# First attention's q and k produced with tokens on the partitions, head norms and rotation along the free axis, moving weights realigned

## The chip, the cores and the metric

The kernel runs on one core of a Trainium2 chip. The metric is the device time of one execution in microseconds. The kernel before took 2663.46 us (median of 3 runs, 2660.84 to 2664.37).

## The reference

Two transformer-like layers follow each other on one sequence of 256 tokens with 2048 features, in float32. What matters here is the first layer's attention. The hidden state is normalised and multiplied by `w_in`; the first 3072 output features are q, k and v, 16 heads of 64 features each. Every head of q and k is normalised and its first 16 features are rotated by an angle that depends on the token:

```
h = rms_norm(x, g_mix)
q, k, v, z, xbc, dt_raw = split(h @ w_in)
q = partial_rope(rms_norm(q, g_q), positions) * 64 ** -0.5      # norm over the 64 features of a head
k = partial_rope(rms_norm(k, g_k), positions)
partial_rope: x1, x2 = x[:8], x[8:16] of each head; [x1*cos - x2*sin, x2*cos + x1*sin, x[16:]]
```

The masked softmax of q k^T over three window patterns follows, then `w_out`. Beside the attention runs a state-space branch (SSD) made from z, xbc and dt. Cross attention, an MLP and the whole second layer come after it.

## The kernel before

**Weights.** All large matmuls go through one stream of 907 granules. A granule is a weight tile of 256 input features by 512 output features (128 partitions x 1024 floats, 512 KB). It is loaded into one of five `raw` buffers seven granules ahead; ScalarE copies it rounded into `WH` (`high`), VectorE writes the rest `raw - WH` into `WL` (`low`, line 1901); both are rings of four slots. The activations have the same two halves, `XH` and `XL`. Each product is three fp32r matmul passes: XH with WH, XL with WH, XH with WL.

**Two forms of a granule** (`gran`, line 933). In the narrow form the weights are stationary (128x128) and the 256 tokens are moving: 24 matmuls of 256 columns; the result has output features on the partitions. In the wide form, used for v, w_cv and v2, the tokens are stationary (two blocks of 128) and 512 weight columns are moving: 12 matmuls of 512 columns; the result has tokens on the partitions. A narrow slot of the ring spreads its 256-float blocks 288 floats apart; a wide one (`flat_slot`, line 702) is contiguous from the slot's start, and slots are 1120 floats apart, so wide weights start at 0, 96, 64 or 32 floats past a multiple of 128.

**Order of work.** `make_plan` (line 324) gives each granule a slot of time and each side step a due slot. `chain` (line 198) places a row of dependent steps in consecutive slots, later when PSUM banks (`B`, four of them) or scratch tiles (`T`, eight) are taken. Each engine's loop goes through the slots, and within a slot through the steps in a fixed written order. On TensorE the granule comes first and then the side steps; on VectorE `low` comes first, then among others softmax steps, `qk_rope`, `qk_gain`, `qk_rs`, `qk_scale`, then `ssm_gain`, `ssm_rs`, `ssd_out`, `ssd_mask`. So each engine waits in its own order, and a step that is late holds everything written behind it.

**q and k before.** Chunks q,0 k,0 v,0 q,1 k,1 v,1 take slots 49 to 96, eight granules each. Per chunk there are two units of 256 features by 256 tokens, eight units j = 0 to 7. A unit's steps: `qk_scale` (VectorE: PSUM times the norm row), `qk_sq` (ScalarE: squares), `qk_sum` (TensorE: four small fp32 matmuls that sum 64 partitions), `qk_rs` (VectorE: inverse root by 12 small operations), `qk_wide` (ScalarE) and `qk_spread` (TensorE: four transposes that spread the roots over the partitions), `qk_gain` (VectorE), `qk_rot` (TensorE: an fp32 matmul of 512 columns with a rotation matrix) and `qk_rope` (VectorE: three operations of 512 elements). The first units stand in slots 57 to 63. The SSD steps stand beside them: the mask of unit 6 (`ssd_mask`) and its two heads' matmuls (`ssd_y`, which wait for it) in slot 58, those of unit 7 in slot 62.

Of the kernel before, what the change touches and what calls it, by code (L numbers as in the profile page):

```python
# [15 lines left out]
RING = 4  # L16
# [3 lines left out]
SLOT = 4 * BLOCK + 3 * 32  # L20
EPS = 1e-6
# [9 lines left out]
def cst_layout():  # L31
    names = [("ident", 128), ("tri", 128), ("ones", 128), ("tri2", 128), ("blk", 2), ("rot64", 128),
             ("dup", 128), ("rotdup", 128),
             ("mult", 384), ("causal", 384), ("invf", 1), ("pad", 3)]
    out, at = {}, 0
    for n, w in names:
        out[n] = (at, w)
        at += w
    return out, at


def col_layout():
    names = [("conv_w", 64), ("conv_b", 16), ("lru_ba", 16), ("lru_bi", 16), ("ffn_wg", 132), ("ffn_bg", 44),
             ("g_mix", 16), ("g_q", 1), ("g_k", 1), ("g_attn_out", 8), ("d_skip", 8),
             ("g_ssm_out", 8), ("g_cross", 16), ("g_mem", 16), ("g_cq", 1), ("g_ck", 1), ("g_mlp", 16),
             ("dt_bias", 16), ("a_log", 16), ("rnn_w", 64), ("rnn_b", 16), ("lru_lam", 16), ("ln1_g", 16),
             ("ln1_b", 16), ("ffn_wu", 132), ("ffn_bu", 44), ("ln2_g", 16), ("ln2_b", 16)]
    out, at = {}, 0
    for n, w in names:
        out[n] = (at, w)  # L50
        at += w
    return out, at
# [6 lines left out]
    "hn_scale": "qk_scale", "hn_rs": "qk_rs", "hn_gain": "qk_gain", "lam_x": "dt_x", "lam_one": "dt_one",  # L59
    "lam_end": "dt_end", "xr_taps": "xbc_taps", "gr_poly": "xs_mul", "gr_gelu": "cb_mask", "gr_mul": "z_scale",  # L60
    "rn_mul": "z_silu", "at_mul": "ssd_mask", "mg_lo": "ms_lo", "up_sq": "ssd_out", "up_lo": "xbc_silu",
    "dn": "xbc_scale", "qi_rope": "qk_rope", "kw_ki": "dt_acs", "rq": "ssm_gain", "lru_la": "ssm_rs",
# [6 lines left out]
    "up_hi": "z_tanh", "gr_sq": "ssd_exp", "gr_tanh": "ssm_sq", "rn_tanh": "ms_hi", "at_tanh": "qk_wide",  # L69
    "gt_tap": "xr_tap", "ln_hi": "rn_tanh", "ix_relu": "rope_sin_act", "lru_sqrt": "rope_cos_act", "ln_meanrow": "mg_hi",  # L70

    "hn_sum": "qk_sum", "hn_spread": "qk_spread", "ln_meanrow_pe": "xs_pe", "qi_rot": "qk_rot", "kw_pe": "dt_rows", "ix_qk": "cb_pe",
# [4 lines left out]
def granules():  # L77
# [33 lines left out]
    for r, (c0, n) in enumerate(ROUNDS):  # L111
# [3 lines left out]
        for c in range(4):  # L115
# [10 lines left out]
         "ssm_spread", "qk_sum", "qk_spread", "qk_rot", "sm_qk", "sm_tr", "sm_av", "hn_sum", "hn_spread", "qi_rot",  # L126
# [197 lines left out]
def make_plan():  # L324
# [231 lines left out]
def program(nc, A):  # L556
# [4 lines left out]
    with ctx:  # L561
# [130 lines left out]
        def slot(x, g):  # L692

            a = (g % RING) * SLOT
            return x[:, a:a + SLOT]

# [5 lines left out]
        def flat_slot(g):  # L702

            return width(g) < GRAN or P.grans[g][0] in ("v", "w_cv", "v2")
# [26 lines left out]
        def width(g):  # L731
            return weights(g)[1]
# [4 lines left out]
        def qk_of(j):  # L737

            return (qT, kT)[j // 2 % 2], 2 * (j // 4) + j % 2
# [30 lines left out]
        def sync(e):  # L770
# [21 lines left out]
            for t in range(P.slots):  # L792
# [32 lines left out]
        def tensor(e):  # L825
# [19 lines left out]
            def pair_over(job, c):  # L845
# [7 lines left out]
                elif job in ("q", "k"):  # L853
                    on.wait_ge(*s("qk_scale", 4 * c + (2 if job == "q" else 4)))
# [78 lines left out]
            def gran(g):  # L933
# [26 lines left out]
                elif job in ("v", "w_cv", "v2"):  # L960
# [120 lines left out]
            def qk_sum(j):  # L1081
                out, sq = S("qk", j), T("qk", j)
                on.wait_ge(*s("qk_sq", j + 1))
                free_S(on, "qk", j)
                for i in range(2):
                    for k in range(2):
                        a = k * 4 + i * 2
                        m = mm(out[:, a:a + 2], sq[:, i * 256 + k * 128:i * 256 + k * 128 + 128], C("blk"))
                m.then_inc(s["qk_sum"], 1)

            def qk_spread(j):
                out, wide = S("qk", j), T("qk", j)
                on.wait_ge(*s("qk_wide", j + 1))
                for i in range(2):
                    for k in range(2):
                        a = k * 4 + i * 2
                        m = tr(out[:, i * 256 + k * 128:i * 256 + k * 128 + 128], wide[:, a * 64:a * 64 + 128])
                m.then_inc(s["qk_spread"], 1)

            def qk_rot(j):  # L1100
                on.wait_ge(*s("qk_gain", j + 1))
                mm(S("qk", j)[:, :], C("rot64"), pair(*qk_of(j))).then_inc(s["qk_rot"], 1)


            def sm_qk(u):
                if u < 8:
                    on.wait_ge(*s("qk_rope", 3 + u // 2 % 2 + 4 * (u // 4)))
# [150 lines left out]
            for t in range(P.slots):  # L1258
# [36 lines left out]
                for u in P("qk_rot", t):  # L1295
                    qk_rot(u)
                for u in P("qk_spread", t):
                    qk_spread(u)
                for u in P("qk_sum", t):
                    qk_sum(u)  # L1300
# [19 lines left out]
        def scalar(e):  # L1320
# [118 lines left out]
            def qk_sq(j):  # L1439
                free_T(on, "qk", j)  # L1440
                on.wait_ge(*s("qk_scale", j + 1))
                fn(T("qk", j)[:, :], pair(*qk_of(j)), ACT.Square).then_inc(s["qk_sq"], 1)

            def qk_wide(j):
                on.wait_ge(*s("qk_rs", j + 1))
                fn(T("qk", j)[:, :].rearrange("p (c d) -> p c d", d=64),
                   root(5 + j % 4)[:, 0:8].unsqueeze(2).to_broadcast([128, 8, 64]), ACT.Copy).then_inc(s["qk_wide"], 1)
# [278 lines left out]
            for t in range(P.slots):  # L1726
# [82 lines left out]
                for u in P("qk_wide", t):  # L1809
                    qk_wide(u)  # L1810
# [75 lines left out]
        def vector(e):  # L1886
# [218 lines left out]
            def rope_angle(_):  # L2105
                a = T("rope")[:, 0:256]
                free_T(on, "rope")
                on.wait_ge(s["pos"], 16)
                e.tensor_copy(a, cosA[:, :].bitcast(I32)).then_inc(*own.up())
                on.wait_ge(*own.now)  # L2110
                ts(a, a, C("invf"), None, ALU.mult).then_inc(s["rope_angle"], 1)

            def reduced(out, turn):

                a, k = T("rope")[:, 0:256], T("rope")[:, 256:512]
# [27 lines left out]
            def qk_scale(j):  # L2143
                x, p = qk_of(j)
                on.wait_ge(s["gemm"], P.count("qk"[j // 2 % 2], j // 4))
                tt(x[:, 2 * p:2 * p + 2, :], two(bank("qk"[j // 2 % 2], j // 4, j % 2)), twice(rb[:, 0, :]),
                   ALU.mult).then_inc(s["qk_scale"], 1)

            def qk_rs(j):
                on.wait_ge(*s("qk_sum", j + 1))  # L2150
                rsqrt(root(5 + j % 4)[:, 0:8], S("qk", j)[:, 0:8], 8, 1.0 / 64, EPS).then_inc(s["qk_rs"], 1)

            def qk_gain(j):
                x = pair(*qk_of(j))
                on.wait_ge(*s("qk_spread", j + 1))
                stt(x, x, V(("g_q", "g_k")[j // 2 % 2]), S("qk", j)[:, :], ALU.mult, ALU.mult).then_inc(s["qk_gain"], 1)
# [410 lines left out]
            for t in range(P.slots):  # L2567
# [108 lines left out]
                for u in P("qk_rope", t):  # L2676
                    qk_rope(u)
# [4 lines left out]
                for u in P("qk_scale", t):  # L2682
                    qk_scale(u)
# [52 lines left out]
def constants():  # L2736
# [14 lines left out]
    put("blk", (i[:, None] // 64 == np.arange(2)[None, :]).astype(np.float32))  # L2751
# [45 lines left out]
    put("invf", table(64, 8)[:, None])  # L2797
# [67 lines left out]
```

## Time and profile before

| | |
|---|---|
| median of 3 runs | 2663.46 us |
| the profiled execution's own time | 2664.01 us |
| its span | 2662.2 us |
| TensorE busy | 2640.7 us |
| VectorE busy | 1775.5 us |
| ScalarE busy | 1337.8 us |
| GpSimd busy | 112.5 us |
| q and k stretch, 158 to 333 us: TensorE, VectorE busy | 174.53, 138.77 us |

Busy time of matmuls is not their rate: they are pipelined, so a matmul that is shown as 0.28 us can start every 0.11 us. The distance from start to start is what counts. A row of the list in order of time has the start, the time covered, engine, line, operation, output <- inputs and, in brackets, idle time ahead of it.

### The profile page before, as it was taken

The page shows a single profiled execution, that of the slowest core. Times are in us where ns is not written, and L with a number is a line of the kernel's source. Part 1 is how long each engine was busy: PE and PEld are TensorE (multiplying, and loading weights), DVE is VectorE, ACT ScalarE, POOL GpSimd, SP SyncE. Part 2 cuts the span into 40 slices and gives each one's busy share as a digit, 9 for nine tenths or more (in the row PEclk, how much of TensorE's full clock was granted, in tenths as well). Part 3 has the DMA queues.
Part 4 walks back from the last instruction along what each step waited for, and adds up shares of the span by engine and source line. Part 5 has one row for each costly group of instructions (what it writes and reads, how often), then busy time and mean ns, then how long its engine had stood idle before and what let it go on. Part 6 is the DMA issues. An engine that isn't in the chain of part 4 may idle for free.

```text
span 2662.2 us, 52796 instructions
## 1 busy us (share of the span) xinstructions
PE 2640.7 (99%) x22474; PEld 2591.6 (97%) x22474; DVE 1775.5 (67%) x2594; ACT 1337.8 (50%) x1817; POOL 112.5 (4%) x76
## 2 busy tenths in 40 slices
PE   9999999999999999999999999999999999999998
PEld 9998899899999999999899999999999999999997
DVE  7787779675555555565787786556676656665666
ACT  6474575554344443444445774444455435543553
POOL 2000021010000000000000000000300000000003
PEclk9999999999999999999999999999999999999999
DMA  7544546466666566665554556665566666666663
GB/s 254 181 143 151 177 157 189 150 207 192 196 192 197 191 195 193 196 192 178 166 167 153 178 180 194 194 195 183 150 199 192 196 193 196 192 196 192 197 191 103
DMA packets 137179, 488.45 MB, mean 183 GB/s; under 512 B 15344, under 2 KB 18288, under 8 KB 136944
## 3 DMA queue, kind: packets, MB, share of 16 engines
q1 hardware_dynamic: 136656, 484.82, 57.8%
q8 instruction: 176, 2.88, 0.5%
q14 instruction: 59, 0.48, 0.1%
q10 hardware_dynamic: 288, 0.26, 0.0%
HBM read 482.93 MB, written 2.10 MB: 182 GB/s over the span
## 4 chain that ended last, share of the span: by engine, by line
PE 94%; DVE 4%; ACT 1%; issue 0%; DMA 0%; SPq 0%; POOL 0%; ACTq 0%; DVEq 0%
PE ps L830 93%; DVE WL L1891 1%; PE ps L833 1%; DVE XL L1899 1%; DVE xT L1891 1%; DMA raw<-in_w_in 0%; ACT WH L1325 0%; DVE T L1891 0%; DVE XL L1891 0%; ACT xT L1325 0%; DVE T L1899 0%; DVE small L1899 0%; SPq L783 0%; DVE AL L1899 0%; ACT XH L1325 0%
## 5 line engine op out<-in xcount | busy, mean ns | idle before, releaser
L1891 DVE TENSOR_TENSOR WL<-raw,WH 128x1024 fp32r<-128x1024 f32 (+1 forms) x910 | 1123.6, 1238 | 755.2 <-ACT WH L1325 754.7
L1325 ACT ACTIVATE WH<-raw 128x1024 fp32r<-128x1024 f32 (+1 forms) x910 | 961.7, 1058 | 1265.0 <-PE ps L830 1261.9
L830 PE MATMUL ps<-XH,WH 128*128 128x256 f32 x5024 | 1401.2, 279 | 5.7 <-DVE WL L1891 3.6
L830 PE MATMUL ps<-XL,WH 128*128 128x256 f32 x5024 | 1389.5, 277 | 0.0
L830 PE MATMUL ps<-XH,WL 128*128 128x256 f32 x5024 | 1389.5, 277 | 0.0
L830 PEld LDWEIGHTS ps<-XH,WH 128*128 128x128 f32 x5024 | 943.1, 188 | 13.0 <-issue 11.6
L830 PEld LDWEIGHTS ps<-XL,WH 128*128 128x128 f32 x5024 | 943.3, 188 | 2.0 <-issue 1.2
L830 PEld LDWEIGHTS ps<-XH,WL 128*128 128x128 f32 x5024 | 942.9, 188 | 0.3
L830 PE MATMUL ps<-AH,WH 128*128 128x256 f32 x1856 | 513.0, 276 | 0.6 <-DVE AL L1891 0.4
L830 PE MATMUL ps<-AL,WH 128*128 128x256 f32 x1856 | 512.3, 276 | 0.0
L830 PE MATMUL ps<-AH,WL 128*128 128x256 f32 x1856 | 512.3, 276 | 0.0
L830 PEld LDWEIGHTS ps<-AH,WH 128*128 128x128 f32 x1856 | 348.4, 188 | 1.0 <-DVE AL L1891 0.6
L830 PEld LDWEIGHTS ps<-AL,WH 128*128 128x128 f32 x1856 | 348.4, 188 | 0.0
L830 PEld LDWEIGHTS ps<-AH,WL 128*128 128x128 f32 x1856 | 348.4, 188 | 0.0
L1842 POOL TENSOR_TENSOR T<-T 128x512 f32<-128x512 f32 (+1 forms) x50 | 77.6, 1555 | 490.6 <-ACT T L1325 489.3
L1842 POOL TENSOR_TENSOR T<-xT 128x512 f32<-128x512 f32 x2 | 2.6, 1308 | 1986.2 <-ACT T L1325 1986.2
L1899 DVE SCALAR_TENSOR_TENSOR T<-ps,cols,T 128x254 f32<-128x254 f32 (+2 forms) x186 | 76.8, 474 | 0.0
L1325 ACT ACTIVATE T<-ps,cols 128x256 f32<-128x256 f32 x120 | 56.5, 529 | 0.0
L1325 ACT ACTIVATE T<-ps 128x512 f32<-128x512 f32 (+2 forms) x110 | 55.7, 536 | 0.1
L830 PE MATMUL ps<-WH,XH 128*128 128x512 f32 x96 | 39.7, 414 | 0.0
L1325 ACT ACTIVATE T<-T 128x256 f32<-128x256 f32 (+1 forms) x94 | 39.7, 470 | 0.1
L830 PE MATMUL ps<-WL,XH 128*128 128x512 f32 x96 | 37.8, 394 | 0.0
(235 smaller groups left out, 1587.0 us busy)
## 6 DMA issues: line engine op xcount, KB each, us to landing
raw<-in_w_up SPq DMA_DIRECT2D x304, 512.0 KB, 4.3
raw<-in_w_in SPq DMA_DIRECT2D x223, 512.0 KB, 3.5
raw<-in_w_down SPq DMA_DIRECT2D x216, 512.0 KB, 4.3
raw<-in_w_out SPq DMA_DIRECT2D x64, 512.0 KB, 3.5
raw<-in_w_gates SPq DMA_DIRECT2D x64, 512.0 KB, 3.5
raw<-in_w_ckv SPq DMA_DIRECT2D x16, 512.0 KB, 3.6
raw<-in_w_cq SPq DMA_DIRECT2D x8, 512.0 KB, 4.4
raw<-in_w_co SPq DMA_DIRECT2D x8, 512.0 KB, 3.3
```

What stands on the lines that cost most here:

```text
L830: return e.matmul(out, l, r, start=start, stop=True, skip_group_check=True)
L833: return e.transpose(out, x, C("ident")[0:n, 0:n])
L1325: return e.activation(out, x, func, **kw)
L1842: return e.tensor_tensor(out, a, b, ALU.add)
L1891: return e.tensor_tensor(out, a, b, op)
L1899: return e.scalar_tensor_tensor(out=out, in0=a, scalar=x, in1=b, op0=op0, op1=op1)
```

## The change

q and k join v in the wide form, so they come out with tokens on the partitions, and a unit becomes 128 tokens by 512 features (8 heads). The sum over a head's 64 features is then a reduction along the free axis, on VectorE; the root is a value per partition and head; the rotation works on the first 16 features of each head, with tables of 32 values instead of 256 per partition. Four transposes bring the unit back to features on the partitions. The step list of a unit shrinks from nine to five. `qk_scale`, `qk_sum`, `qk_wide`, `qk_spread`, `qk_rot` and `qk_rope` are gone, `qk_tr` and `qk_copy` are new. The start of a wide slot of full size moves by `FLAT_AT`, so that it is 96 floats past a multiple of 128 in all four ring slots, for v, w_cv and v2 as well. The constants and columns tables change size (1670 to 1680 and 748 to 874 floats per partition), which shifts every tile placed behind them.

```
+FLAT_AT = (96, 0, 32, 64)
...
-        rope.append(P.chain(t, j, ("qk_scale", "qk_sq", "qk_sum", "qk_rs", "qk_wide", "qk_spread", "qk_gain", "qk_rot",
-                                   "qk_rope"),
-                            (T, ("qk", j), "qk_sq", "qk_rope"), (B, ("qk", j), "qk_sum", "qk_rope")))
+        rope.append(P.chain(t, j, ("qk_sq", "qk_rs", "qk_gain", "qk_tr", "qk_copy"),
+                            (T, ("qk", j), "qk_sq", "qk_tr"), (B, ("qk", j), "qk_tr", "qk_copy"), apart=("qk_tr",)))
...
+            if flat_slot(g) and width(g) == GRAN:
+                a += FLAT_AT[g % RING]
+                return x[:, a:a + GRAN]
...
-            return width(g) < GRAN or P.grans[g][0] in ("v", "w_cv", "v2")
+            return width(g) < GRAN or P.grans[g][0] in ("q", "k", "v", "w_cv", "v2")
...
-                    on.wait_ge(*s("qk_scale", 4 * c + (2 if job == "q" else 4)))
+                    on.wait_ge(*s("qk_gain", 4 * c + (2 if job == "q" else 4)))
...
+            def qk_tr(j):
+                out, y = S("qk", j), T("qk", j)
+                on.wait_ge(*s("qk_gain", j + 1))
                 free_S(on, "qk", j)
+                for i in range(4):
+                    m = tr(out[:, i * 128:i * 128 + 128], y[:, i * 128:i * 128 + 128])
+                m.then_inc(s["qk_tr"], 1)
...
             def qk_sq(j):
+                _, x, t = qk_of(j)
                 free_T(on, "qk", j)
+                on.wait_ge(*s("norm_rs", 1))
+                on.wait_ge(s["gemm"], P.count("qk"[j // 2 % 2], j // 4))
+                fn(T("qk", j)[:, :], x[:, :], ACT.Square, scale=rcol[:, t:t + 1]).then_inc(s["qk_sq"], 1)
+
+            def qk_copy(j):
+                out, _, _ = qk_of(j)
+                on.wait_ge(*s("qk_tr", j + 1))
+                fn(out, S("qk", j)[:, :].rearrange("p (f t) -> p f t", f=4), ACT.Copy).then_inc(s["qk_copy"], 1)
...
             def qk_rs(j):
+                r, t = root(5 + j % 4), qk_of(j)[2]
+                on.wait_ge(*s("qk_sq", j + 1))
+                e.tensor_reduce(r[:, 8:16], T("qk", j)[:, :].rearrange("p (h d) -> p h d", d=64), AX_X,
+                                ALU.add).then_inc(*own.up())
+                on.wait_ge(*own.now)
+                rsqrt(r[:, 0:8], r[:, 8:16], 8, 1.0 / 64, EPS).then_inc(*own.up())
+                on.wait_ge(*own.now)
+                ts(r[:, 0:8], r[:, 0:8], rcol[:, t:t + 1], None, ALU.mult).then_inc(s["qk_rs"], 1)
...
             def qk_gain(j):
+                _, x, t = qk_of(j)
+                y, r, g = T("qk", j), root(5 + j % 4), V(("g_q", "g_k")[j // 2 % 2], 0, 64)
+                on.wait_ge(*s("qk_rs", j + 1))
+                for h in range(8):
+                    m = stt(y[:, 64 * h:64 * h + 64], x[:, 64 * h:64 * h + 64], r[:, h:h + 1], g, ALU.mult, ALU.mult)
+                m.then_inc(*own.up())
+                on.wait_ge(*own.now)
+                on.wait_ge(*s("rope_sin_act", 1))
+                on.wait_ge(*s("rope_cos_act", 1))
+                y = y[:, :].rearrange("p (h d) -> p h d", d=64)
+                by_cos, by_sin = (turn[:, n, :].rearrange("p (h d) -> p h d", d=16) for n in range(2))
+                for by, angle in ((by_cos, cosA), (by_sin, sinA)):
+                    row = angle[:, 16 * t:16 * t + 16].unsqueeze(1).to_broadcast([128, 8, 16])
+                    m = tt(by, y[:, :, 0:16], row, ALU.mult)
+                m.then_inc(*own.up())
+                on.wait_ge(*own.now)
+                tt(y[:, :, 0:8], by_cos[:, :, 0:8], by_sin[:, :, 8:16], ALU.subtract)
+                tt(y[:, :, 8:16], by_cos[:, :, 8:16], by_sin[:, :, 0:8], ALU.add).then_inc(s["qk_gain"], 1)
...
-                e.dma_start(cosA[:, :].bitcast(I32), A["pos"].to_broadcast([128, 256])).then_inc(s["pos"], 16)
+                e.dma_start(cosA[:, 0:2].bitcast(I32), A["pos"]).then_inc(s["pos"], 16)
```

## Rows read from the trace of the kernel before

**Rows 1.** The page's busy times, shares of the span and instruction counts.
```profile
PE 2640.7 (99%) x22474; PEld 2591.6 (97%) x22474; DVE 1775.5 (67%) x2594; ACT 1337.8 (50%) x1817; POOL 112.5 (4%) x76
```
**Rows 2.** By windows: stretch, length, busy time of each engine, clock, DMA.
```profile
158.00:333.00 175.00, 174.53 (x1290) 155.15 (x1289) 138.77 (x344) 94.56 (x164) 0.00 (x0) 1.00 0.50 159
```
**Rows 3.** TensorE in order of time, 474 to 482 us: start, covered, what.
```profile
474.06 0.28 PE L830 MATMUL ps<-XH,WH 128*128 128x256 f32 x1
...
476.77 0.39 PE L830 MATMUL ps<-WH,AH 128*128 128x512 f32 x1
...
479.52 0.39 PE L830 MATMUL ps<-WH,AH 128*128 128x512 f32 x1
...
482.31 0.94 PE L830 MATMUL ps<-cst,T 128*128 128x1 f32 x8
```
**Rows 4.** TensorE in order of time around three side blocks of q and k.
```profile
197.51 0.28 PE L830 MATMUL ps<-XH,WL 128*128 128x256 f32 x1
197.62 0.95 PE L830 MATMUL ps<-cst,T 128*128 128x2 f32 x8
...
198.63 0.28 PE L830 MATMUL ps<-XL,WH 128*128 128x256 f32 x1
...
231.78 0.39 PE L830 MATMUL ps<-WL,XH 128*128 128x512 f32 x1
232.01 0.60 PE L833 MATMUL ps<-cst,T 128*128 128x128 f32 x4
...
232.68 0.39 PE L830 MATMUL ps<-WH,XL 128*128 128x512 f32 x1
...
239.06 0.40 PE L830 MATMUL ps<-WL,XH 128*128 128x512 f32 x1
239.29 1.02 PE L830 MATMUL ps<-kT,cst 128*128 128x512 f32 x2
...
240.39 0.40 PE L830 MATMUL ps<-WH,XL 128*128 128x512 f32 x1
```
**Rows 5.** VectorE in order of time: a root chain, then rotation and gain.
```profile
194.52 0.16 DVE L1896 TENSOR_SCALAR small<-ps 128x8 f32<-128x8 f32 x1
...
196.82 0.98 DVE L1899 SCALAR_TENSOR_TENSOR T<-xbc,cols,ps 64x256 f32<-64x256 f32 x2
...
205.76 1.22 DVE L1891 TENSOR_TENSOR WL<-raw,WH 128x1024 fp32r<-128x1024 f32 x1
206.89 0.68 DVE L1891 TENSOR_TENSOR T<-ps,sinA 128x512 f32<-128x512 f32 x1
...
208.82 0.74 DVE L1899 SCALAR_TENSOR_TENSOR qT<-qT,cols,ps 128x512 f32<-128x512 f32 x1
209.48 0.86 DVE L1899 SCALAR_TENSOR_TENSOR zT<-zT,cols,ps 128x256 f32<-128x256 f32 x2
```
**Rows 6.** VectorE's groups, whole span: count, busy us, mean ns, idle before.
```profile
L2182 DVE TENSOR_REDUCE small<-ps 128x2 f32<-128x512 f32 x4 | 2.8, 692 | 1.3 <-PE ps L830 1.3
...
L1899 DVE SCALAR_TENSOR_TENSOR dts<-ps,rcol,cols 128x16 f32<-128x16 f32 x2 | 0.4, 229 | 0.6 <-PE ps L833 0.6
```
**Rows 7.** VectorE in order of time at slots 57 and 58.
```profile
188.44 0.99 DVE L1899 SCALAR_TENSOR_TENSOR T<-xbc,cols,ps 64x256 f32<-64x256 f32 x2
189.47 0.43 DVE L1899 SCALAR_TENSOR_TENSOR zT<-T,zT 128x256 f32<-128x256 f32 x1
189.81 1.22 DVE L1891 TENSOR_TENSOR WL<-raw,WH 128x1024 fp32r<-128x1024 f32 x1
191.06 0.69 DVE L1891 TENSOR_TENSOR qT<-ps,rb 128x512 f32<-128x512 f32 x1
191.67 0.86 DVE L1899 SCALAR_TENSOR_TENSOR zT<-zT,cols,ps 128x256 f32<-128x256 f32 x2
192.45 1.02 DVE L1891 TENSOR_TENSOR P<-P,cbm 128x384 f32<-128x384 f32 x2
```
**Rows 8.** TensorE in order of time: the matmuls that wait for that mask.
```profile
193.99 0.87 PE L830 MATMUL ps<-P,xsd 128*64 128x256 f32 x8
```
**Rows 9.** By windows, 24 to 32 us, columns as in rows 2.
```profile
24.00:32.00 8.00, 5.96 (x38) 5.79 (x38) 8.00 (x5) 4.15 (x6) 7.69 (x5) 0.79 0.90 321
```

More of the change, by code:

```diff
@@ L31, in cst_layout @@
 def cst_layout():
[L32 removed]
+    names = [("ident", 128), ("tri", 128), ("ones", 128), ("tri2", 128), ("rot64", 128),
              ("dup", 128), ("rotdup", 128),
[L34 removed]
+             ("mult", 384), ("causal", 384), ("invf", 16)]
     out, at = {}, 0
@@ L57 @@
 SHARED = {
-    "hn_scale": "qk_scale", "hn_rs": "qk_rs", "hn_gain": "qk_gain", "lam_x": "dt_x", "lam_one": "dt_one",
+    "hn_rs": "qk_rs", "hn_gain": "qk_gain", "lam_x": "dt_x", "lam_one": "dt_one",
     "lam_end": "dt_end", "xr_taps": "xbc_taps", "gr_poly": "xs_mul", "gr_gelu": "cb_mask", "gr_mul": "z_scale",
     "rn_mul": "z_silu", "at_mul": "ssd_mask", "mg_lo": "ms_lo", "up_sq": "ssd_out", "up_lo": "xbc_silu",
-    "dn": "xbc_scale", "qi_rope": "qk_rope", "kw_ki": "dt_acs", "rq": "ssm_gain", "lru_la": "ssm_rs",
+    "dn": "xbc_scale", "kw_ki": "dt_acs", "rq": "ssm_gain", "lru_la": "ssm_rs",
     "lru_m": "rope_angle", "lru_scan": "rope_sin", "tk_start": "rope_cos", "gt_taps": "xr_taps", "ln_lo": "mg_lo",
@@ L959, in gran @@
                                    k == 0 and i == 0 and p == 0)
-                elif job in ("v", "w_cv", "v2"):
+                elif job in ("q", "k", "v", "w_cv", "v2"):
                     for t in range(2):
@@ L1078, in ssm_spread @@
                 m.then_inc(s["ssm_spread"], 1)
-            def qk_sum(j):
-                out, sq = S("qk", j), T("qk", j)
-                on.wait_ge(*s("qk_sq", j + 1))
+            def qk_tr(j):
+                out, y = S("qk", j), T("qk", j)
+                on.wait_ge(*s("qk_gain", j + 1))
                 free_S(on, "qk", j)
[L1085 to L1102, printed above, removed]
+                for i in range(4):
+                    m = tr(out[:, i * 128:i * 128 + 128], y[:, i * 128:i * 128 + 128])
+                m.then_inc(s["qk_tr"], 1)
             def sm_qk(u):
                 if u < 8:
-                    on.wait_ge(*s("qk_rope", 3 + u // 2 % 2 + 4 * (u // 4)))
+                    on.wait_ge(*s("qk_copy", 4 + 4 * (u // 4)))
                 elif u < 12:
@@ L1294, in tensor @@
                     hn_sum(u)
[L1295 to L1300, printed above, removed]
+                for u in P("qk_tr", t):
+                    qk_tr(u)
                 for u in P("ssm_spread", t):
@@ L1808, in scalar @@
                     ca_hi(u)
-                for u in P("qk_wide", t):
-                    qk_wide(u)
+                for u in P("qk_copy", t):
+                    qk_copy(u)
                 for u in P("rope_cos_act", t):
@@ L2105, in rope_angle @@
             def rope_angle(_):
-                a = T("rope")[:, 0:256]
+                a, p = T("rope")[:, 0:32], T("rope")[:, 64:66]
                 free_T(on, "rope")
                 on.wait_ge(s["pos"], 16)
-                e.tensor_copy(a, cosA[:, :].bitcast(I32)).then_inc(*own.up())
+                e.tensor_copy(p, cosA[:, 0:2].bitcast(I32)).then_inc(*own.up())
                 on.wait_ge(*own.now)
-                ts(a, a, C("invf"), None, ALU.mult).then_inc(s["rope_angle"], 1)
+                for t in range(2):
+                    m = ts(a[:, 16 * t:16 * t + 16], C("invf"), p[:, t:t + 1], None, ALU.mult)
+                m.then_inc(s["rope_angle"], 1)
             def reduced(out, turn):
-                a, k = T("rope")[:, 0:256], T("rope")[:, 256:512]
+                a, k = T("rope")[:, 0:32], T("rope")[:, 32:64]
                 full, most = 2.0 * np.pi, 3.1415925
@@ L2141, in rope_cos @@
                 reduced(cosA[:, :], 0.25).then_inc(s["rope_cos"], 1)
[L2143 to L2147, printed above, removed]
-            def qk_rs(j):
-                on.wait_ge(*s("qk_sum", j + 1))
-                rsqrt(root(5 + j % 4)[:, 0:8], S("qk", j)[:, 0:8], 8, 1.0 / 64, EPS).then_inc(s["qk_rs"], 1)
@@ L2796, in constants @@
         tab += [np.cos(ang), sin]
-    put("invf", table(64, 8)[:, None])
+    put("invf", np.tile(inv(8, 16), 2)[None, :])
     return c, np.stack(tab, axis=1).astype(np.float32)
@@ L2826 @@
     parts = {
-        "g_mix": col(I["g_mix"]), "g_q": np.tile(I["g_q"].reshape(64), 2)[:, None],
-        "g_k": np.tile(I["g_k"].reshape(64), 2)[:, None], "g_attn_out": col(I["g_attn_out"]),
+        "g_mix": col(I["g_mix"]), "g_q": every(I["g_q"]), "g_k": every(I["g_k"]),
+        "g_attn_out": col(I["g_attn_out"]),
         "conv_w": col(I["conv_w"]), "conv_b": col(I["conv_b"]), "d_skip": col(np.repeat(I["d_skip"].reshape(16), 64)),
```

38 lines of the change are left out of this document (10 added, 28 removed).

## The prediction

> **What bounds the kernel now.** I read the page's busy shares first: TensorE is busy 2640.7 of 2662.2 us, VectorE 67% of the span [rows 1]. Time can therefore come off only where TensorE gets less to do, and is lost only where it starts to wait. The change works in about 158 to 333 us; the table by windows has TensorE busy 174.53 of those 175 us at full clock, and VectorE 138.77 [rows 2]. So no wait is waiting to be removed there. A busy TensorE says nothing of how fast it goes, so next I read its instructions in order of time and take start-to-start distances.
>
> **Weight matmuls.** Before a granule of q or k is 24 matmuls with 256 moving columns; after it is 12 with 512. 24 of the narrow ones take 476.77 - 474.06 = 2.71 us, 12 wide ones 479.52 - 476.77 = 2.75 us and, in the next ring slot, 482.31 - 479.52 = 2.79 us [rows 3]. The two wide granules differ in where the weights start: 96 floats past a multiple of 128 for the first (229 ns each), 64 for the second (233 ns). The change gives every full wide slot the offset 96. q and k: 32 x (2.75 - 2.71) = +1.3 us. v, w_cv and v2: 16 of their 32 granules sit at 0 or 64 and save 0.04 us each, 8 more about 0.01: -0.8 us. Together +0.5 us. Bounds: if the good place is lost (larger tables ahead move all big tiles by 544 bytes), q and k are at 2.79 and the others win nothing, +2.6 us; from below, if the offset that is good in rows 3 is not yet the best, twice the step between the two rows, 0.08 us on each of 64 wide granules, -5 us.
> The rows show that the position of the moving weights changes the rate, 229 against 233 ns. The Trainium skill, TensorE: Matmul & The Clock Gate, section Step-by-step, says that loading the next stationary tile takes no SBUF bandwidth from the running matmul, and section Back-to-back issue gap would by its N / 2.4 + 2.5 price a wide one at 216 ns. By the first rule realigning gives nothing (+1.3 us instead of +0.5), by the second the wide form would already be 0.15 us a granule faster than it is; rows 3 stand against both.
>
> **Side work taken off TensorE.** For each of the 8 units (q or k, half c, 128 tokens after, 256 features before) three blocks stand between granules. A block's price is the start of the second weight matmul behind it less the start of the last one ahead of it, less two normal distances. Sums: 198.63 - 197.51 - 0.23 = 0.89 us. Spread (4 transposes): 232.68 - 231.78 - 0.46 = 0.44. Rotation matmul: 240.39 - 239.06 - 0.46 = 0.87 [rows 4]. Removed: 2.20 us. Added: 4 transposes of 128x128, the same operation as the spread, 0.44. Net 8 x 1.76 = -14.1 us, all on the path.
>
> **VectorE's work.** Before, a unit costs it scale 0.61 (191.67 - 191.06 [rows 7]), the root chain 196.82 - 194.52 = 2.30, gain 209.48 - 208.82 = 0.66, rotation 208.82 - 206.89 = 1.93 [rows 5]: 5.5 us in five slots. After, the first step, qk_rs, is one tensor_reduce of 512 elements (busy 0.69, and a dependent one starts 0.03 later: 0.73 [rows 6]), the same chain 2.30, and a dependent multiply, about 0.2: 3.2 us in one piece. qk_gain is 8 multiplies of 64 columns: a 16-column one is busy 0.23 [rows 6], of which some 0.08 overlaps its follower, a 512-column one 0.66 apart; linear between, 0.20 each, 1.6 us; then two of 128 elements and two of 64, about 0.95 with their waits: 2.55 us. Per unit 5.75 us, only 0.25 more, but in two lumps. ScalarE loses one 512-column copy and gains one, so nothing; the rotation tables shrink eightfold, which takes 2 to 3 us off VectorE at slots 44 to 48, hidden since TensorE never waited there.
>
> **Where the lumps land.** Slots are the planner's. New due slots, for a unit whose chunk is ready at t: square t, root t+1, gain t+2, transposes t+3, copy t+4; first units at 57 and 58. VectorE works strictly in the code's order: in a slot the low half of the weights, gain, root, then the SSD steps. In the stretch of k,0 it is already full: rows 7 follow each other without a gap. PSUM is booked for shorter, so the last SSD unit moves forward: its mask and y from slot 62 to 60, and the last ssm norm from 66 to 64.
> Slot 58: today scale 191.06, ssm gain 191.67, mask 192.45 to 193.4, and the two heads' matmuls that wait for it start at 193.99 [rows 7, 8]. After: the root step (3.2) stands where the scale (0.61) was. The low half ahead of it starts at 189.81 and takes 1.13 (206.89 - 205.76 [rows 5]); so roots from 190.95, ssm gain 0.78, mask 0.95, which ends at 195.9. TensorE, without the sums, is ready at 193.1: it waits 2.75 us.
> Slot 59 on VectorE: low half 1.13, gain 2.55, roots 3.2, the SSD step of slot 59 1.37 (189.81 - 188.44 [rows 7]): 8.25, to 204.1; slot 60: 1.13 + 2.55 + 0.95, mask 7 ends at 208.75. TensorE after its stop: 195.9 + y 0.9 + spread 0.45 = 197.25, two granules 202.7, transposes and ssm sums 204.0: it waits 4.75 us for mask 7. The matmuls and transposes queued behind that wait, and the ring of weights, move with it.
> Units 2 and 3. With these stops slot 65 begins for TensorE at 222.1, and VectorE waits there for the sums of the last ssm norm; its root chain ends at 224.4. Then VectorE: low 1.13, roots 3.2, ssm gain 0.8, low 1.13, gain 2.55, roots 3.2, low 1.13, gain 2.55, end 240.1. TensorE: granules 65 to 68, a small spread and the first transposes, 233.8, granule 69, 236.6: it waits 3.5 us.
> Units 4 and 5, from the start of slot 82 for both: VectorE at low and softmax norm 1.45, roots 4.65, then 1.13, 2.55, 3.2 and 0.6 for the SSD output's low half, 12.15, then 1.13, softmax maximum 1.3, gain 2.55, 17.15. TensorE: four granules 11.0 (slots 82 to 85), side blocks 0.65, 1.85, 0.44, is at 14.15: it waits 3.0 us. Units 6 and 7 have no softmax beside them: VectorE, which starts 1.35 ahead, ends at 13.35, TensorE is there at 11.45: 1.9 us.
> Sum of the five waits 15.9, less some 0.3 us of wait that the chip shows in this stretch today (175 - 174.53 = 0.47 in all [rows 2]): +15.6 us. Low bound: if the new steps cost half a microsecond less each and the SSD unit stays where it was, about 5 us; high bound: 0.5 more each, 22 us. I take 15.6.
>
> **Clock.** A wait of TensorE is followed by lost speed: in the stretch 24 to 32 us TensorE stands still for 2.0 us, and the granted clock over those 8 us is 0.79, so between the two levels, 2.4 and 1.2 GHz; 0.21 x 8 = 1.7 us [rows 9]. The five waits lie between bounds of 0 (shorter waits, some work between) and 5 x 1.7 = 8.5. I take one such loss, behind the longest wait: +1.7 us.
> **Start.** The cols table grows by 64 KB, positions are 8-byte pieces, and the raw tiles' addresses lose a 256-byte boundary. Bounds -0.5 to +2, taken as 0: the weights lie seven granules ahead outside the first 30 us. The Trainium skill, DMA: Bandwidth & Descriptors, section How a descriptor splits into AXI transactions, would give a 4 KB piece 17 transactions instead of 16; no run here shows what the write side pays.
>
> **Sum** against the profiled execution, 2664.0 us (span 2662.2 and 1.8 around it): -14.1 + 0.5 + 15.6 + 1.7 = +3.7, 2667.7. The median of the three runs, 2663.5, is 0.5 us lower; so 2667.
>
> **Rivals.** A, the matmuls go and the waits do not come: VectorE's small operations overlap better than I count, or TensorE's cover takes the lumps. For: a low half made at 189.81 is used only from about 198.4 [rows 7, 4], a lead of over 7 us. Against: the lead covers weight tiles, not a step that waits for VectorE in its own slot, as mask 7 does. It gives 2663.5 - 13.6 + 3 left over = 2653. B, waits cost more: each above 2 us drops the clock, and the lumps are 0.5 us dearer each: +22 + 5 - 13.6 = +13, 2677. It decides from the point where TensorE stands still at mask 7 for more than 5 us; today mask 6 ends at 193.4 and its matmuls start at 193.99, behind the sums [rows 8]. C, the address shift of 544 bytes changes the distance of all 21,408 weight matmuls: a tenth of the 4 ns that an offset makes in a wide one, 0.4 ns each, is 8.6 us, either sign; for it only that distances depend on offsets at all [rows 3], against it that relative offsets within the narrow form are kept and all of its slots run alike.
>
> **How the numbers follow.** A measurement tells some 0.2%, 5.3 us, from no change. Forecast (gain and waits cancel within 5 us) 0.42; A 0.30; B 0.20; C 0.08, half each way. Faster is A, half of C and a little of the forecast's edge: 0.35; slower is B and the other half: 0.25; same 0.40. Its own range for the forecast is 2660 to 2673; the 8 in 10 range reaches into A and B: 2650 to 2675.
>
> **What would show it.** Right: waits of TensorE on VectorE's P (masks) of some 7 us in two places and on T (the transposes' input) of 8 us in three between 190 and 330 us; a copy of q and k after them; blocks of 8 sums and rotation gone; wide granules all at 2.75 us. A is right if TensorE stays above 99% busy there. Wrong altogether: a narrow distance other than 113.3 ns, or waits elsewhere than in these five slots.

## The result, and the profile after

The changed kernel takes 2675.48 us (median of 4 runs, 2671.09 to 2677.29); beside it the kernel before took 2663.08 us. The ratio is 1.0046, 95% interval 1.0034 to 1.0059: slower by 12.4 us, where 2667 (2650 to 2675) was forecast. A second set gave 2676.58 us and 1.0049 (1.0036 to 1.0061).

The page's busy line of the changed kernel, which answers to [rows 1], and the windows, columns as in [rows 2]; the first of them answers to that row.

```profile
PE 2630.5 (99%) x22010; PEld 2566.2 (96%) x22010; DVE 1772.6 (66%) x2667; ACT 1337.3 (50%) x1817; POOL 110.7 (4%) x76
```
```profile
158.00:333.00 175.00, 158.76 (x779) 125.50 (x778) 134.54 (x404) 90.00 (x156) 0.00 (x0) 0.95 0.43 146
185.00:224.00 39.00, 32.92 (x157) 26.31 (x154) 31.34 (x103) 16.49 (x27) 0.00 (x0) 0.87 0.33 111
224.00:252.00 28.00, 24.54 (x116) 19.33 (x115) 23.21 (x80) 9.87 (x12) 0.00 (x0) 1.00 0.42 144
279.00:313.00 34.00, 29.33 (x142) 22.86 (x141) 25.75 (x83) 19.19 (x41) 0.00 (x0) 0.90 0.39 128
```

In these 175 us TensorE now stands still for 16.2 us instead of 0.5: 174.53 us busy before, 158.76 now, at a granted clock of 0.95 instead of 1.00. The work that the change takes off it, forecast as 14.1 us, is hidden in these numbers, because at the lower clock the same work keeps it busy for longer. VectorE is less busy than before, so its total explains nothing.

The profiled execution of the changed kernel is the shortest of its runs, 2671.09 us. The second profile of the same kernel (2676.42 us) is nearer to the median, and both are used below.

TensorE in order of time, changed kernel, the rows that have idle time of 2 us or more in brackets. Five of them, in 190 to 330 us:

```profile
194.67 0.87 PE L835 MATMUL ps<-P,xsd 128*64 128x256 f32 x8 [2.92 <-DVE P L1879]
...
207.57 1.55 PE L835 MATMUL ps<-P,xsd 128*64 128x256 f32 x8 [3.15 <-DVE P L1879]
...
241.45 0.66 PE L838 MATMUL ps<-cst,T 128*128 128x128 f32 x4 [3.46 <-DVE T L1879]
...
296.79 1.08 PE L838 MATMUL ps<-cst,T 128*128 128x128 f32 x4 [4.67 <-DVE small L1883]
...
328.87 0.66 PE L838 MATMUL ps<-cst,T 128*128 128x128 f32 x4 [2.04 <-DVE T L1879]
```

Together 16.2 us. Read the first number in the brackets as the price, and the second number of the row (time covered) as a hint at the clock: the same eight matmuls cover 0.87 us at full clock, as in [rows 8], and 1.55 us after the second wait. What stands behind the first wait shows it better. TensorE, changed kernel, from 196 us:

```profile
196.24 0.78 PE L835 MATMUL ps<-WH,XH 128*128 128x512 f32 x1
196.81 0.63 PE L835 MATMUL ps<-WH,XL 128*128 128x512 f32 x1
...
198.52 0.54 PE L835 MATMUL ps<-WL,XH 128*128 128x512 f32 x1
198.90 0.40 PE L835 MATMUL ps<-WH,XH 128*128 128x512 f32 x1
199.13 0.40 PE L835 MATMUL ps<-WH,XL 128*128 128x512 f32 x1
```

Up to 198.52 the starts are 0.43 us apart (four distances in 1.71 us), from 198.90 on 0.23: the lower level, 1.2 GHz, lasts half a granule behind the wait and costs that granule 1.1 us. As the price of the lower clock I take, for each granule, the mean distance of its matmuls less 229 ns, times 12.

VectorE of the changed kernel at slots 58 and 59, which answers to [rows 5, 7]. The root step of unit 0 runs from 189.41 to 192.81 (3.40 us, forecast 3.2) and stands ahead of the ssm gain and the mask; the gain step runs from 195.67 to 198.13 (2.46, forecast 2.55):

```profile
189.41 0.68 DVE L2136 TENSOR_REDUCE small<-T 128x8 f32<-128x512 f32 x1
...
192.81 0.87 DVE L1887 SCALAR_TENSOR_TENSOR zT<-zT,cols,ps 128x256 f32<-128x256 f32 x2
193.60 1.02 DVE L1879 TENSOR_TENSOR P<-P,cbm 128x384 f32<-128x384 f32 x2
...
195.67 1.62 DVE L1887 SCALAR_TENSOR_TENSOR T<-ps,small,cols 128x64 f32<-128x64 f32 x8
...
198.13 0.68 DVE L2136 TENSOR_REDUCE small<-T 128x8 f32<-128x512 f32 x1
```

The longest wait, at 296.79, is not for the gain of unit 5, as forecast. Unit 4's transposes take over a PSUM bank that a softmax maximum frees, and on VectorE that maximum stands behind unit 4's gain and unit 5's root step:

```profile
287.78 1.62 DVE L1887 SCALAR_TENSOR_TENSOR T<-ps,small,cols 128x64 f32<-128x64 f32 x8
...
290.24 0.68 DVE L2136 TENSOR_REDUCE small<-T 128x8 f32<-128x512 f32 x1
...
295.25 0.28 DVE L2184 CUSTOM_DVE_ANT_0 P<-ps,cst 128x128 f32<-128x128 f32 x1
```

Two things came as forecast. A narrow distance is still 113.3 ns, and behind the last place of the table below the two profiles need 2243.8 us before and 2244.1 after, so rival C is out, and the transposes of a unit take 203.46 - 203.03 = 0.43 us:

```profile
203.03 0.60 PE L838 MATMUL ps<-cst,T 128*128 128x128 f32 x4
203.46 0.28 PE L835 MATMUL ps<-cst,T 128*128 128x1 f32 x2
```

### The profile page after: what moved, and what is told of

Same layout as the page of the kernel before. It is cut to its first block, busy times and chain, and to the rows that moved or that the text cites. A ratio compares the mean times of both kernels' runs of the same rounds, so it can differ in the third digit from the quotient of the medians.

```text
span 2669.3 us, 51932 instructions
## 1 busy us (share of the span) xinstructions
PE 2630.5 (99%) x22010; PEld 2566.2 (96%) x22010; DVE 1772.6 (66%) x2667; ACT 1337.3 (50%) x1817; POOL 110.7 (4%) x76
## 4 chain that ended last, share of the span: by engine, by line
PE 92%; DVE 6%; ACT 1%; issue 0%; DMA 0%; SPq 0%; POOL 0%; ACTq 0%; DVEq 0%
PE ps L835 91%; DVE WL L1879 2%; PE ps L838 1%; DVE XL L1887 1%; DVE T L1887 1%; DVE xT L1879 1%; ACT WH L1311 0%; DVE small L1887 0%; DMA raw<-in_w_in 0%; DVE T L1879 0%; DVE XL L1879 0%; ACT xT L1311 0%; DVE small L1879 0%; ACT P L1311 0%; DVE small L2136 0%
## 5 line engine op out<-in xcount | busy, mean ns | idle before, releaser
L835 PE MATMUL ps<-XH,WH 128*128 128x256 f32 x4768 | 1326.6, 278 | 7.1 <-DVE WL L1879 4.5
L835 PE MATMUL ps<-XL,WH 128*128 128x256 f32 x4768 | 1317.7, 276 | 0.0
L835 PE MATMUL ps<-XH,WL 128*128 128x256 f32 x4768 | 1317.6, 276 | 0.0
L835 PEld LDWEIGHTS ps<-XH,WH 128*128 128x128 f32 x4768 | 893.7, 187 | 12.7 <-issue 11.6
L835 PEld LDWEIGHTS ps<-XL,WH 128*128 128x128 f32 x4768 | 893.7, 187 | 1.8 <-issue 1.0
L835 PEld LDWEIGHTS ps<-XH,WL 128*128 128x128 f32 x4768 | 893.7, 187 | 0.3
L835 PE MATMUL ps<-WH,XH 128*128 128x512 f32 x224 | 92.8, 414 | 0.0
L835 PE MATMUL ps<-WH,XL 128*128 128x512 f32 x224 | 89.4, 399 | 0.0
L835 PE MATMUL ps<-WL,XH 128*128 128x512 f32 x224 | 89.2, 398 | 0.0
```

The costliest lines, as they stand in the source:

```text
L835: return e.matmul(out, l, r, start=start, stop=True, skip_group_check=True)
```

## Experiments

All times are medians beside runs of the kernel before on the same chip, with the ratio's 95% interval. A common measure for all traces: the first matmul of chunk q,0 and the first of the third chunk of w_out_a stand 407.24 - 158.06 = 249.18 us apart before, and everything that the change touches but v2 and w_cv lies between. What a kernel differs in from 249.18 is free of the chance of the start. "Waits" are those of TensorE there, the last column is the lower clock's cost as defined above.

| kernel | median us | difference us | waits us | granules at the lower clock: number, cost us |
|---|---|---|---|---|
| changed, first profile | 2675.48 | +8.37 | 16.2 | 3, 4.5 |
| after_again | 2676.58 | +11.19 | 15.1 | 5, 7.9 |
| fill | 2670.12 | +5.86 | 19.4 (14.7 filled) | 0 |
| fill_one | 2673.34 | +9.64 | 16.8 (4.5 filled) | 3, 5.6 |
| order | 2672.32 | +9.05 | 16.8 | 3, 4.2 |
| late | 2667.03 | +4.40 | 13.9 | 2, 3.7 |
| order_late | 2667.76 | +4.44 | 13.3 | 2, 4.2 |
| spread | 2652.58 | -10.45 | 3.2 | 0 |
| spread_only | 2653.59 | -10.47 | 3.6 | 0 |
| spread_late | 2652.59 | -9.20 | 3.4 | 1, 1.8 |
| spread_order | 2652.36 | -9.83 | 2.7 | 1, 1.7 |

The last column leaves out the side blocks that run at the lower clock. The work removed (-14.1), the wide form in the stretch (+0.6), the waits less the 0.5 us of before, and this column add up to +9.0 of the +11.19 of after_again and to +5.4 of the +5.86 of fill, where nothing is slow.

**after_again**, no edit.

> The changed kernel once more, beside the kernel before on the same chip. Both theories: about 2675 us, ratio 1.0046. Its profile gives the base for the others: five waits of TensorE in 190 to 330 us, 16.3 us in all, and a granted clock under 0.95 in 185:224 and 279:313. Theory 'lumps and clock': these two rows are there again (clock loss of 8 to 9 us in the two windows together less what the waits themselves are). Rival 'clock is chance': the waits are the same, and the windows' clock is 1.00 in this profile.

2676.58 us, ratio 1.0049 (1.0036 to 1.0061). The waits are the same within 1.2 us, the clock is not: now 224:252 has lost some too.

```profile
185.00:224.00 39.00, 34.09 (x166) 27.05 (x164) 31.44 (x102) 16.57 (x27) 0.00 (x0) 0.87 0.33 108
224.00:252.00 28.00, 24.54 (x111) 19.21 (x111) 22.13 (x80) 10.38 (x12) 0.00 (x0) 0.94 0.43 144
279.00:313.00 34.00, 29.32 (x140) 22.84 (x139) 26.25 (x88) 18.59 (x39) 0.00 (x0) 0.90 0.36 118
```

A granule at the lower clock follows each of the five waits here, three of them in the first profile. So whether a wait of 2 to 3.5 us costs clock is chance from run to run, and the median run probably has more losses than the first profile, the shortest of its set. The rival fell: both windows are below 0.95 again.

**fill** puts work for nothing ahead of the five waits:

```
+FILL_Y = {6: 5, 7: 6}
+FILL_TR = {3: 7, 4: 10, 7: 4}
...
+            def fill(out, n):
+                a = CL["ident"][0]
+                for _ in range(n):
+                    mm(out[:, 0:256], C("ones"), cst[:, a:a + 256])
```

> Ahead of each of the five waits TensorE gets 4 to 10 matmuls of ones by the identity (fp32, 256 columns, about 0.4 us each, result overwritten), in a bank that is free already, so that it works while it waits; the order of all else is unchanged. Theory 'the clock falls because TensorE stands still': the starts of the real work behind a wait stay where they were, the clock in the windows behind them goes to 1.00, and 5 to 8 us come back: about 2669. Rival 'the clock is not part of it, the waits are the whole price': the time stays within 1 us of the changed kernel, 2675, or rises by what the fill overshoots (up to 0.4 us a place).

2670.12 us, ratio 1.0022 (1.0013 to 1.0031): 6.5 us less than after_again. Each of these fp32 matmuls shows as two passes in the rows, five of them as x10. TensorE of this kernel at the first wait: ten passes of fill from 193.24, 0.76 us of wait left, and behind it the granule at 0.23 us a matmul, not 0.43.

```profile
193.24 2.32 PE L837 MATMUL ps<-cst 128*128 128x256 f32 x10
196.32 0.87 PE L837 MATMUL ps<-P,xsd 128*64 128x256 f32 x8 [0.76 <-DVE P L1895]
...
198.07 0.40 PE L837 MATMUL ps<-WL,XH 128*128 128x512 f32 x1
198.30 0.40 PE L837 MATMUL ps<-WH,XH 128*128 128x512 f32 x1
```
```profile
185.00:224.00 39.00, 35.45 (x190) 28.51 (x189) 31.30 (x103) 17.07 (x27) 0.00 (x0) 1.00 0.32 110
...
279.00:313.00 34.00, 33.26 (x168) 26.17 (x167) 25.74 (x84) 20.50 (x42) 0.00 (x0) 1.00 0.39 136
```

The theory held. It also shows what the waits are worth at full clock: from TensorE's arrival to the real work 3.08, 3.68, 3.61, 4.86 and 2.18 us, and two new ones of 0.93 and 1.02 us: 19.4 us. Behind each fill TensorE still waits for 0.30 to 0.84 us, so no fill ran past the end of its wait. In the changed kernel TensorE comes later to its next wait because it is slow behind the last one, which hides some 3 us of them.

**fill_one** keeps only the fill ahead of unit 4's transposes (`FILL_Y = {}`, `FILL_TR = {4: 10}`).

> The changed kernel with the fill of 20 passes of 256 columns (4.5 us) only ahead of unit 4's transposes, where TensorE waits longest (4.7 us). Theory 'each wait has a clock loss of its own behind it': the clock in 279:313, 0.90, goes to 1.00 and 2 to 3 of the 6.4 us that the five fills brought come back: 2673 to 2674.5. Rival 'the clock falls once and for the stretch': 0 or the whole 6.4.

2673.34 us, ratio 1.0038 (1.0026 to 1.0051): 3.2 us less than after_again, in another set, with overlapping intervals, so the time alone does not show a gain. The windows do. The window with the filled wait is at full clock, the ones with unfilled waits are not:

```profile
185.00:224.00 39.00, 32.94 (x158) 26.19 (x157) 31.21 (x102) 16.21 (x26) 0.00 (x0) 0.87 0.32 107
224.00:252.00 28.00, 24.54 (x106) 19.51 (x105) 21.33 (x74) 9.65 (x11) 0.00 (x0) 0.88 0.39 133
...
279.00:313.00 34.00, 33.29 (x174) 25.97 (x171) 26.97 (x93) 19.92 (x42) 0.00 (x0) 1.00 0.37 123
```

The losses belong to the single waits: the filled one has none, and three of the four others are followed by one (1.3 to 1.9 us of distances over the normal one), the last, of 2.04 us, by none.

**order** moves the two VectorE loops behind the SSD steps and holds the last SSD unit:

```
+                for u in P("z_scale", t):
+                    z_scale(u)
+                for u in P("qk_gain", t):
+                    qk_gain(u)
+                for u in P("qk_rs", t):
+                    qk_rs(u)
...
-        t = max(t, (z0, z0 + 1, z - 1, z)[u // 2] + 1)
+        t = max(t, (z0, z0 + 1, z - 1, z)[u // 2] + 1, 60 if u == 7 else 0)
```

> In VectorE's order qk_gain and qk_rs go behind the ssm and SSD steps of the slot, and the last SSD unit is held where it was before the change (mask and y in slot 62, not 60). Theory 'lumps': the two mask waits (2.9 and 3.15 us) go, and with them the clock loss behind them (5.1 us in 185:224), less what the transposes of units 0 and 1 now wait: 6 to 10 us off, 2665 to 2669. Rival 'VectorE is simply full there': the wait only moves to the transposes of units 0 to 2, and the time stays at 2673 to 2676.

2672.32 us, ratio 1.0035 (1.0021 to 1.0048). No mask wait is left, but the waits of TensorE in 158 to 340 us (line, releaser: total, times, longest) sum to the same:

```profile
PE ps L838 <- DVE T L1879: 9.4, 4, 3.7
PE ps L838 <- DVE small L1883: 4.7, 1, 4.7
PE ps L838 <- DVE small L1887: 2.7, 1, 2.7
```

I expected 6 to 10 us and got 4. The rival was nearer: VectorE's order only chooses who waits. How much of the 4 us is chance of the clock stays open.

**late** gives the transposes a slot more, by an argument `late=("qk_tr",)` of `chain` that adds one slot ahead of that step.

> The planner puts the transposes (and the copy) one slot later behind the gain, about 2.8 us of cover. Theory 'lumps': the waits of the transposes in slots 69, 84/85 and 93 (3.5, 4.7 and 2.0 us) shrink by 2.8 each at most, 7 of the 10.2 us, and half of the clock loss goes (3.4 us in 279:313): 2665 to 2668. The two mask waits stay or are dearer. Rival 'a bank held one slot longer costs as much': the wait turns into one for a free PSUM bank, and the time stays at 2673 to 2678.

2667.03 us, ratio 1.0013 (1.0005 to 1.0022). The waits on T (5.5 us) are gone, the bank wait stays at 4.8, and mask 7 is dearer, 5.1 instead of 3.2 or 2.0:

```profile
PE ps L835 <- DVE P L1879: 8.0, 2, 5.1
PE ps L838 <- DVE small L1883: 4.8, 1, 4.8
```

The time is the one expected and 9.5 us below after_again in the same set, though the waits are only 1 to 2 us shorter in sum (13.9 against 15.1 and 16.2). In the profile they are fewer, and two granules are slow instead of five (3.7 us against 7.9). Of the 6.8 us by which the stretch is shorter (11.19 - 4.40) 1.2 are waits, the rest is clock.

**order_late** has both edits.

> Both edits of the runs order and late together. Theory 'lumps on VectorE in adjacent slots': the mask waits are gone as in order, the transposes of units 0 to 3 and 6, 7 are covered, and what stays is the bank that unit 4's transposes take over from a softmax maximum behind two root steps (4.7 us) with its clock loss: 2656 to 2661. Rival 'VectorE is full around slots 58 to 62': the masks' wait only moves on to the next thing that needs VectorE, 5 to 8 us there as in both, and the time is 2664 to 2667, no better than late alone (2667.0).

2667.76 us, ratio 1.0018 (1.001 to 1.0027), no better than late alone. The rival was right. The masks' wait moved to the row that spreads the ssm norm, in one piece:

```profile
PE ps L838 <- DVE small L1887: 7.3, 1, 7.3
PE ps L838 <- DVE small L1883: 4.8, 1, 4.8
```

Neither order nor cover takes these waits away while two units pass through VectorE in adjacent slots.

**spread** adds to order_late a table of distances between units:

```
+QK_AT = (0, 4, 0, 4, 0, 4, 0, 2)
...
-        t = E("qkqk"[j // 2], j // 4) + 1 + j % 2
+        t = E("qkqk"[j // 2], j // 4) + 1 + QK_AT[j]
```

> As order_late, and the second unit of each q or k chunk takes its five steps four slots behind the first (the last one two), not one, so that VectorE has one root or gain step in a slot and gets even with TensorE between. Theory 'two lumps in adjacent slots make the waits': waits of TensorE in 158 to 340 us are under 4 us in all, the clock there stays at 1.00, and of the 14.1 us taken off TensorE 10 to 13 arrive: 2650 to 2654, below the kernel before. Rival 'VectorE lacks the time altogether' (5.75 us a unit, 11.5 a chunk of 22 us, beside 9 of low halves): waits of 8 us or more stay, 2660 or above.

2652.58 us, ratio 0.9964 (0.9952 to 0.9977). The waits are 3.2 us, and no granule behind them is at the lower clock. Of the 14.1 us taken off TensorE 9.9 arrive, just under the 10 to 13 expected.

**spread_only** is the changed kernel with this table alone.

> The changed kernel with one edit: the second unit of a chunk comes four slots behind the first (the last one two). Order of VectorE's steps, transposes and the SSD unit as in the changed kernel. Theory 'two lumps in adjacent slots make the waits': the waits of 3.5 us (transposes of unit 3) and 4.7 us (bank behind the softmax maximum) go with their clock loss, mask 7's (2.0 to 3.2) goes, mask 6's (2.9) stays, since only unit 0's root step stands ahead of it: 2655 to 2659. Rival 'the other two edits of spread did it': 2665 or above.

2653.59 us, ratio 0.9966 (0.9953 to 0.9978): 9 us faster than before and 22 to 23 faster than the changed kernel, by two edited lines. Its longest wait (two short ones, 0.7 us, are left out), and its windows:

```profile
PE ps L836 <- DVE P L1880: 2.9, 1, 2.9
...
```
```profile
185.00:224.00 39.00, 35.39 (x182) 28.34 (x181) 36.11 (x125) 18.48 (x29) 0.00 (x0) 1.00 0.41 131
...
279.00:313.00 34.00, 34.00 (x176) 27.00 (x175) 32.36 (x111) 20.49 (x40) 0.00 (x0) 1.00 0.62 217
```

VectorE does the same steps; in 279:313 it is busy 32.36 us instead of 25.75, since it works where it waited for TensorE and the weights behind it, and since other steps fall into the window. In its order of time unit 4's root (284.19), a softmax maximum (289.20) and unit 4's gain (290.51) now follow each other with low halves between, and unit 5's root comes only at 297.51:

```profile
284.19 0.68 DVE L2137 TENSOR_REDUCE small<-T 128x8 f32<-128x512 f32 x1
...
289.20 0.28 DVE L2185 CUSTOM_DVE_ANT_0 P<-ps,cst 128x128 f32<-128x128 f32 x1
...
290.51 1.62 DVE L1888 SCALAR_TENSOR_TENSOR T<-ps,small,cols 128x64 f32<-128x64 f32 x8
...
297.51 0.68 DVE L2137 TENSOR_REDUCE small<-T 128x8 f32<-128x512 f32 x1
```

It came out better than expected, since mask 6's wait of 2.9 us, which stayed, cost no clock in this profile.

The table moves more than the second units. The planner starts the first half's softmax behind unit 3 (`rope[3] + 1`), so its steps come three slots later too: the maximum that held unit 4's bank in slot 84 is now in slot 87. No run separates the two. For the waits at the masks and at the transposes of units 3 and 7 (slots 60, 69 and 93) no softmax step is involved, so there the distance alone is left; of the 4.7 us of the bank it is not shown which of the two took them away.

**spread_late** and **spread_order** are spread_only with one of the other edits each.

> spread_only and the transposes one slot later; VectorE's order and the SSD unit as in the changed kernel. By the theory the masks decide what is left, not the transposes: mask 6's 2.9 us with one clock loss behind it stays, and the rest is covered: 2654 to 2657, about 2 us better than spread_only and 3 behind spread. Rival 'the order is the larger part': over 2660.

> spread_only with the order edit (gain and root behind the SSD steps, the last SSD unit held), the transposes not later. By the theory no mask wait; the transposes come 1 slot behind a gain that now ends later, so waits of 1 to 3 us before some of the 8: 2655 to 2660. Rival 'a slot is cover enough once the lumps are apart': same as spread, 2652.6.

2652.59 us (0.9964, 0.995 to 0.9977) and 2652.36 us (0.9961, 0.9949 to 0.9974). All four spread kernels lie within 1.3 us and can't be told apart; what they share is the table of distances (and the later softmax). The differences between them that I had expected (2 to 8 us) were too large.

**unaligned** is the changed kernel with `FLAT_AT = (0, 0, 0, 0)`.

> The changed kernel with the wide granules' weights where the ring slots put them (offsets 0, 96, 64 and 32 floats past a multiple of 128), not all at 96. Theory 'position sets the rate': half of the 64 wide granules at 233 ns a matmul and a quarter at 230, so 32 x 0.048 + 16 x 0.012 = +1.7 us on the changed kernel, about 2678; q's and k's granules in these slots are 2.79 us apart. Rival 'the 4 ns belong to the stage, not to the position': all at 229, no difference.

2679.24 us, ratio 1.0062 (1.0049 to 1.0076), whose interval overlaps that of after_again; the time alone does not decide. The rows do. TensorE of this kernel, two granules of q one behind the other, the first with weights at 96 floats past a multiple of 128, the second at 64:

```profile
158.17 0.39 PE L835 MATMUL ps<-WH,XL 128*128 128x512 f32 x1
...
160.69 0.39 PE L835 MATMUL ps<-WH,XH 128*128 128x512 f32 x1
...
163.25 0.39 PE L835 MATMUL ps<-WL,XH 128*128 128x512 f32 x1
```

Eleven distances take 2.52 us in the first and 2.56 in the second, 229 and 233 ns. Over the undisturbed granules of q, k and v (eleven distances each) the means by ring slot are 232.4 and 232.7 ns at offsets 0 and 64, 229.1 and 229.3 at 96 and 32; in the changed kernel all slots are at 228.8 to 229.1. The Trainium skill, TensorE: Matmul & The Clock Gate, section Step-by-step: what each phase is for, says that loading the next tile's weights takes no SBUF read bandwidth from the running matmul. It says nothing of where the moving operand starts, so these rows and [rows 3] add to it and do not stand against it, as the prediction had it.

**before_aligned** gives the kernel before only the new start of v's, w_cv's and v2's wide slots.

> The kernel before with only the realignment of the wide slots (v, w_cv and v2, 32 granules; q and k stay narrow). Theory: -0.8 us, 2662.3, no wait and no clock loss; wide granules of every slot at 229 ns. Rival 'moving these tiles costs elsewhere' (the ring's transfers or copies): 1 us or more above before.

2662.06 us against 2662.46, ratio 0.9999 (0.999 to 1.0008): not to be told from no change, as 0.8 us can't be. In its trace v,0 and v,1 are 0.16 us shorter each, w_cv and v2 too: 0.65 us in all, forecast 0.8.

## Why the prediction was wrong

**Side work, -14.1.** Right. In spread_only the stretch is 10.47 us shorter; with 3.6 us of waits, 0.5 that went, and 0.6 for the wide form (1.0 on q and k, -0.4 on v) that leaves -10.5 - 3.6 + 0.5 - 0.6 = -14.2.

**Wide form and realignment, +0.5.** Right: 32 x 0.03 - 0.65 = +0.3.

**VectorE's prices, 3.2 and 2.55.** Measured 3.40 and 2.46.

**Waits, +15.6.** The sum looks exact in the profile, 16.2 against the 15.9 of the five places, and that is luck. At full clock, as fill shows, it is 19.4. By place, forecast against fill: mask 6 2.75 and 3.08; mask 7 4.75 and 3.68; unit 3 3.5 and 3.61; slots 84 and 85 3.0 (TensorE's terms there add up to 13.94, not 14.15, so 3.2 by the prediction's own prices) and 4.86; units 6 and 7 1.9 and 2.18; two of about 1 us not seen. The step that failed in its kind is that of slots 82 to 85: I followed the transposes to the gain ahead of them, and left out that unit 4's also take a bank, which is freed by a step behind another unit's root. Less the 0.5 us that stood there before, the term is 18.9, 3.3 too small.

**Clock, +1.7.** This is the step that failed most. One loss has about the size that I took from [rows 9]: 0.6 to 2.3 us in after_again, 1.6 on the mean. But I took one, "behind the longest wait", without a reason for one, and there are three to five. The five fills bring back 6.5 us of the median. So 6.5 for 1.7, +4.8 on the forecast, and with the waits +8.1 of the 8.5 us by which it missed. The Trainium skill, TensorE: Matmul & The Clock Gate, section HAM oscillation — how this bites in real kernels, tells of a kernel whose wait in every round of its loop drops the clock again. The traces here agree that several waits cost several losses (five in after_again, 7.9 us), but not that every wait does (three of five in the first profile).

**Start, 0.** Nothing stands against it: q,0 begins at 158.06 us before, at 156.41 and 158.21 in the two profiles of the changed kernel.

**The sum, made again** for the median run: -14.1 + 0.3 + 19.4 - 0.5 + 6.5 = +11.6, measured +12.4.

**The rivals.** B was the nearest in time (2677) and in half of its mechanism: several waits drop the clock, if not each of them. Its other half, lumps dearer by 0.5 us each, did not come (3.40 for 3.2, 2.46 for 2.55), nor did its condition: mask 7 stands at 3.2 us, 3.7 in fill, not over 5. It had 0.20, and the range ended 0.5 us short of the result. A names a place that exists: what it gives, 2653, is what the spread kernels reach, but it takes the other distances between the units for that.

## What to carry to other kernels

Work taken off the full engine comes back as waits if what replaces it on another engine comes in lumps longer than the cover of one slot; its sum may be smaller than before and say nothing. Follow the in-order engine through the slots with two lumps in adjacent ones first, and ask of each waiting step both for its input and for its buffer. When the waits were there, moving VectorE's order left them at 17 us, and a slot more of cover took away 1 to 3; setting the units apart, which moved the softmax too, took 13. Count the waits as well as their sum: late had nearly as much waiting as the changed kernel in fewer pieces and was 9.5 us faster. Price a wait of TensorE at its length and, as a chance, one loss of clock of 0.6 to 2.3 us behind it. In the profiles of the changed kernel and its variants all eight unfilled waits above 4.5 us were followed by a loss, and 14 of the 23 between 1.9 and 3.8 us.

## What the runs showed of the hardware

- The clock loss behind a wait is not a matter of the wait alone. Up to 194 us TensorE and VectorE have the same work in the same order in spread_only and in the changed kernel, and both wait 2.92 us for mask 6. Behind it the changed kernel's matmuls start 0.43 us apart (rows above), those of spread_only 0.23. spread_late is like both up to there and waits 2.94 us; its matmuls start 0.43 us apart again. First spread_only, then spread_late:

```profile
194.31 0.87 PE L836 MATMUL ps<-P,xsd 128*64 128x256 f32 x8 [2.92 <-DVE P L1880]
...
196.30 0.39 PE L836 MATMUL ps<-WH,XH 128*128 128x512 f32 x1
196.53 0.39 PE L836 MATMUL ps<-WH,XL 128*128 128x512 f32 x1
```
```profile
194.18 0.87 PE L836 MATMUL ps<-P,xsd 128*64 128x256 f32 x8 [2.94 <-DVE P L1880]
...
196.19 0.63 PE L836 MATMUL ps<-WL,XH 128*128 128x512 f32 x1
196.62 0.63 PE L836 MATMUL ps<-WH,XH 128*128 128x512 f32 x1
```

  In spread_order even a wait of 1.51 us (at 199.49) has slow matmuls behind it. What decides was not tried.
- Matmuls whose result is thrown away keep the clock: 6.5 us for some 14.7 us of them in the waits.
- The start differs from run to run before any of this work: the second chunk begins at 34.03 us in the profile of before, at 31.97 in before_aligned and at 31.84 to 34.34 in the others. From there to 158 us all traces agree within 0.2 us. So the start alone gives 2.5 us of the 4.1 us by which the runs of one kernel spread (2661.02 to 2665.1 us in 21 runs of before), and the table above measures from q,0. Behind the stretch the profiles differ by another 2.3 us (2242.5 to 2244.8), whose cause stays open; the table leaves that out as well.
